# Causal attention with values and their remainders as one 128-column stationary operand, and the output stored tile by tile

## What is computed

```python
def nsa_attention(q_rope, q_plain, k_cmp, v_cmp, k_slc, v_slc, k_win, v_win, gates):
    ...
    def block(i):
        ...
        s_c = jnp.einsum('bghqd,bgcd->bghqc', qp, k_cmp)
        p_c = jax.nn.softmax(jnp.where(vis_c, s_c, -1e30), axis=-1) * vis_c.astype(f32)
        o_c = jnp.einsum('bghqc,bgcd->bghqd', p_c, v_cmp)
        ...
        s_s = jnp.einsum('bghqd,bgqkd->bghqk', qr, k_g)
        p_s = jax.nn.softmax(jnp.where(vis_s[:, :, None], s_s, -1e30), axis=-1)
        o_s = jnp.einsum('bghqk,bgqkd->bghqd', p_s, v_g)
        ...
        s_w = jnp.einsum('bghqd,bgkd->bghqk', qr, kw)
        p_w = jax.nn.softmax(jnp.where(vis_w, s_w, -1e30), axis=-1)
        o_w = jnp.einsum('bghqk,bgkd->bghqd', p_w, vw)
        return gt[..., 0:1] * o_c + gt[..., 1:2] * o_s + gt[..., 2:3] * o_w
...
def second_block(...):
    ...
        x_lat = x_lat + m_lat[:, 5] * rms_norm_2(sqrelu_mlp(h, mlp_w1[i], mlp_w2[i]), norm_g[i, 3])
    ...
    return x_lat
```

## Time and profile before

| | before |
|---|---|
| median of 3 runs | 3649.59 us (3646.3 to 3649.65) |
| the profiled execution | 3647.38 us, of which its span is 3645.6 us |
| TensorE matmuls | 3450.7 us busy, 95% of the span, 17972 instructions |
| TensorE weight loads | 2851.2 us, 78% |
| VectorE | 1940.6 us, 53% |
| ScalarE | 1360.0 us, 37% |
| GpSimd | 561.3 us, 15% |

### The profile page before, as it was taken

The page is one execution under the profiler, slowest core; times in us unless marked ns, Lnnn a source line. Parts: engine busy times, 40 slices in busy tenths (PEclk is TensorE's granted clock), DMA queues, the critical chain, the costliest instruction groups (busy, mean ns, idle before and its releaser), DMA issues. The chain is left out here.

```text
span 3645.6 us, 46669 instructions
## 1 busy us (share of the span) xinstructions
PE 3450.7 (95%) x17972; PEld 2851.2 (78%) x17972; DVE 1940.6 (53%) x2402; ACT 1360.0 (37%) x1991; POOL 561.3 (15%) x394
## 2 busy tenths in 40 slices
PE   6989999999998999999998999899999999999998
PEld 5766878888776687788876888788888788868886
DVE  4264348777526433877765652533333656654444
ACT  3266234444326623444433443312212344432222
POOL 0042004333104200333320110100000100000000
PEclk9999999999998999999998999999999999999999
DMA  3201234443220032344410001111111011112231
GB/s 127 84 1 58 93 105 145 157 158 115 88 84 1 35 105 93 131 158 160 150 52 18 18 12 70 47 58 65 62 59 68 24 68 52 55 35 93 92 102 60
DMA packets 59364, 287.77 MB, mean 79 GB/s; under 512 B 10704, under 2 KB 11984, under 8 KB 31952
## 3 DMA queue, kind: packets, MB, share of 16 engines
q1 hardware_dynamic: 59216, 285.77, 22.7%
HBM read 283.64 MB, written 2.10 MB: 78 GB/s over the span
## 5 line engine op out<-in xcount | busy, mean ns | idle before, releaser
L162 PE MATMUL ps<-h_hi,w_hi_rest 128*128 128x512 f32 (+1 forms) x1072 | 385.2, 359 | 4.6 <-DVE h_lo L386 4.6
L163 PE MATMUL ps<-h_lo,w_hi_rest 128*128 128x512 f32 (+1 forms) x1072 | 363.4, 354 | 0.0
L1343 POOL TENSOR_TENSOR ada_context<-ada_context,ada_scaled 128x768 f32<-128x768 f32 x112 | 287.5, 2567 | 455.2 <-ACT ada_scaled L1425 450.0
L165 PE MATMUL ps<-h_hi,w_lo_rest 128*128 128x512 f32 (+1 forms) x1072 | 322.0, 355 | 0.0
L151 DVE TENSOR_TENSOR w_lo_mix<-w_raw,w_hi_mix 128x2048 fp32r<-128x2048 f32 x94 | 217.1, 2309 | 185.4 <-ACT w_hi_mix L145 185.4
L425 POOL TENSOR_TENSOR x<-x,y 128x512 f32<-128x512 f32 (+1 forms) x32 | 64.5, 2016 | 1522.3 <-DVE y L431 1522.3
L162 PE MATMUL ps<-h_hi,w_hi_mix 128*128 128x512 f32 x736 | 287.0, 390 | 4.5 <-DVE w_lo_mix L151 2.3
L163 PE MATMUL ps<-h_lo,w_hi_mix 128*128 128x512 f32 x736 | 286.5, 389 | 0.0
L165 PE MATMUL ps<-h_hi,w_lo_mix 128*128 128x512 f32 x736 | 286.5, 389 | 0.0
L1507 DVE TENSOR_TENSOR y<-ps,y 128x512 f32<-128x512 f32 (+1 forms) x224 | 165.7, 751 | 216.1 <-PE ps L165 215.3
L145 ACT ACTIVATE w_hi_rest<-w_raw 128x2048 fp32r<-128x2048 f32 x81 | 154.5, 1908 | 326.7 <-PE ps L165 315.5
(11 more groups left out here) (397 smaller groups left out, 7739.6 us busy)
## 6 DMA issues: line engine op xcount, KB each, us to landing
w_raw<-in_stream SPq DMA_DIRECT2D x205, 1024.0 KB, 5.0
ada_raw<-in_ada_w SPq DMA_DIRECT2D x128, 384.0 KB, 5.1
cmp_w<-in_cmp_w SPq DMA_DIRECT2D x8, 1024.0 KB, 7.3
mla_raw<-in_stream SPq DMA_DIRECT2D x8, 512.0 KB, 3.7
x<-in_x SPq DMA_DIRECT2D x1, 2048.0 KB, 8.9
out<-x SPq DMA_DIRECT2D x1, 2048.0 KB, 7.3
x<-in_ctx SPq DMA_DIRECT2D x1, 1024.0 KB, 11.1
consts<-in_consts SPq DMA_DIRECT2D x1, 768.0 KB, 11.7
```

What stands on the lines that cost most here:

```text
L162: pe.matmul(out, whi, xhi, start=start, stop=False)
L163: pe.matmul(out, whi, xlo, start=False, stop=False)
L165: last = pe.matmul(out, wlo, xhi, start=False, stop=stop)
L1343: pool.tensor_tensor(ada.context, ada.context, ada.scaled[:, j % 2, :], ALU.add).then_inc(m["context"], 1)
```

## The change

Four edits. (1) The values and their remainders become one stationary operand `vp` of 128 columns, 64 of high part and 64 of remainder, and so `values` needs two matmuls a quarter instead of three; rows 0 to 63 of the bank gather what the high parts give, rows 64 to 127 what the remainders give. (2) The compressed branch alike: `pct` becomes F32R with 64 rows, the high part in rows 0 to 31 and the remainder in rows 32 to 63, and `vc_pack` is a stationary operand of the same 64 rows; VectorE makes the remainders in stage_cmp_attention. (3) Once a head the lower half of the bank is rounded into `low_half` by ScalarE (`round_low`) and added to the upper half by a matmul with the identity (`fold`); `head_high` moves two iterations back and `head_low` as well, from iteration 8k+6 to 8k+8. (4) Each of the 8 row tiles is stored by its own DMA as soon as it is added, inside the last residual stage. The diff, cut to its core:

```diff
--- before.py
+++ after.py
...
         k.sem(f"ca_{s}") for s in ("scored", "masked", "exp", "probs", "flipped", "chain"))
     q_hi, q_lo, k_hi, v_hi, v_lo = (k.sem(f"ca_{s}") for s in ("q_hi", "q_lo", "k_hi", "v_hi", "v_lo"))
+    copied, zeroed = k.sem("ca_copied"), k.sem("ca_zeroed")
+    low = slice(NCP, 2 * NCP)
+    def turned(t, g, rows):
+        a = t * 512 + 2048 * g
+        return (b.pct[rows, 4 * g:4 * g + 4, t * P:(t + 1) * P],
+                k.ps[0:NCP, a:a + 512].rearrange("p (h q) -> p h q", q=P))
...
+                pe.wait_ge(zeroed, 1)
                 pe.wait_ge(probs, t // 2 + 1)
                 for h in range(HEADS):
                     a = t * 512 + 2048 * (h // 4) + h % 4 * P
-                    last = pe.transpose(k.ps[0:NC, a:a + P], b.pc[:, t, h, 0:NC], k.c["ident"])
+                    last = pe.transpose(k.ps[0:NCP, a:a + P], b.pc[:, t, h, :], k.c["ident"])
                 last.then_inc(flipped, 1)
...
             normalise(1)
+            for t in range(QT):
+                for g in range(2):
+                    dve.wait_ge(copied, 2 * t + g + 1)
+                    dst, src = turned(t, g, low)
+                    hi, _ = turned(t, g, slice(0, NCP))
+                    dve.tensor_tensor(dst, src, hi.bitcast(F32), ALU.subtract)
...
             def copy(t):
                 act.wait_ge(flipped, t + 1)
                 for g in range(2):
-                    a = t * 512 + 2048 * g
-                    act.activation(b.pct[0:NC, 4 * g:4 * g + 4, t * P:(t + 1) * P],
-                                   k.ps[0:NC, a:a + 512].rearrange("p (h q) -> p h q", q=P), ACT.Copy)
+                    dst, src = turned(t, g, slice(0, NCP))
+                    act.activation(dst, src, ACT.Copy).then_inc(copied, 1)
...
-            act.activation(b.vhi, b.v, ACT.Copy).then_inc(v_hi, 1)
+            by_branch = b.v.rearrange("p t (r d) -> p t r d", d=64)
+            act.activation(b.vp[:, :, :, 0:64], by_branch, ACT.Copy).then_inc(v_hi, 1)
+            act.wait_ge(zeroed, 2)
+            act.activation(b.vcp[0:NC, 0:64], b.vc[0:NC, :], ACT.Copy).then_inc(v_hi, 1)
+            act.activation(b.vcp[NCP:NCP + NC, 0:64], b.vc[0:NC, :], ACT.Copy).then_inc(v_hi, 1)
...
         @block.gpsimd
         def _(pool):
+            pool.memset(b.pc[:, :, :, NC:NCP], 0.0).then_inc(zeroed, 1)
+            pool.wait_ge(zeroed, 1)
+            pool.memset(b.vcp.bitcast(F32), 0.0).then_inc(zeroed, 1)
+            pool.wait_ge(zeroed, 2)
             pool.wait_ge(v_hi, 1)
-            pool.tensor_tensor(b.vlo, b.v, b.vhi.bitcast(F32), ALU.subtract).then_inc(v_lo, 1)
-            pool.wait_ge(v_lo, 1)
+            pool.tensor_tensor(b.vp[:, :, :, 64:P], b.v.rearrange("p t (r d) -> p t r d", d=64),
+                               b.vp[:, :, :, 0:64].bitcast(F32), ALU.subtract).then_inc(v_lo, 1)
+            pool.wait_ge(v_hi, 3)
+            for n, rows in enumerate((slice(0, NC), slice(NCP, NCP + NC))):
+                pool.wait_ge(v_lo, n + 1)
+                pool.tensor_tensor(b.vcp[rows, 64:P], b.vc[0:NC, :], b.vcp[0:NC, 0:64].bitcast(F32),
+                                   ALU.subtract).then_inc(v_lo, 1)
+            pool.wait_ge(v_lo, 3)
             for h in range(HEADS):
                 own, other = head_rows(h)
                 pool.wait_ge(q_hi, h + 1)
...
@@ -866,18 +894,23 @@
                 if br == 0 and part == 0:
                     if h >= 2:
                         pe.wait_ge(s["lo_done"], h - 1)
-                    pe.matmul(k.ps[0:64, bank:bank + 512], b.vc[0:NC, :], b.pct[0:NC, h, :], start=True, stop=True)
+                    pe.matmul(k.ps[:, bank:bank + 512], b.vcp, b.pct[:, h, :], start=True, stop=True)
                 if part == 0:
                     pe.wait_ge(s["pt_lo"], QT * (u + 1))
-                out = k.ps[0:64, bank + j * P:bank + 512]
+                out = k.ps[:, bank + j * P:bank + 512]
                 hi, lo = b.pt[u % 2]
-                vhi, vlo = b.vhi[:, j, 64 * br:64 * br + 64], b.vlo[:, j, 64 * br:64 * br + 64]
-                pe.matmul(out, vhi, hi[:, j, j * P:SEQ], start=False, stop=True, skip_group_check=True)
-                pe.matmul(out, vlo, hi[:, j, j * P:SEQ], start=False, stop=True, skip_group_check=True)
-                last = pe.matmul(out, vhi, lo[:, j, j * P:SEQ], start=False, stop=True,
+                pe.matmul(out, b.vp[:, j, br, :], hi[:, j, j * P:SEQ], start=False, stop=True, skip_group_check=True)
+                last = pe.matmul(out, b.vp[:, j, br, :], lo[:, j, j * P:SEQ], start=False, stop=True,
                                  skip_group_check=True)
                 if j == 0:
                     last.then_inc(s["summed"], 1)
+            def fold(h):
+                bank = VALUES + (h % 2) * 512
+                pe.wait_ge(s["rounded"], h + 1)
+                pe.matmul(k.ps[0:64, bank:bank + 512], b.identr[64:P, 64:P], b.low_half[64:P, :], start=False, stop=True,
+                          skip_group_check=True).then_inc(s["folded"], 1)
...
             for i in range(AHEAD):
                 scores(i)
@@ -887,8 +920,11 @@
                 flips(i)
                 if i >= QT + 1:
                     values((i - QT - 1) // QT, (i - QT - 1) % QT)
+                if i % (2 * QT) == QT + 2 and i > 2 * QT:
+                    fold(i // (2 * QT) - 1)
...
                 values((i - QT - 1) // QT, (i - QT - 1) % QT)
+            fold(HEADS - 1)
...
                 if i + AHEAD < STEPS:
                     top(i + AHEAD)
                 low(i)
-                if i % (2 * QT) == QT + 2 and i > 2 * QT:
-                    head_low(i // (2 * QT) - 1)
+                if i % (2 * QT) == 0 and i > 2 * QT:
+                    head_low(i // (2 * QT) - 2)
+            head_low(HEADS - 2)
             head_low(HEADS - 1)
...
             def head_high(h):
                 bank, rows = VALUES + (h % 2) * 512, slice(64 * (h % 2), 64 * (h % 2) + 64)
+                act.wait_ge(s["folded"], h + 1)
+                act.activation(b.onhi[rows, h // 2, :], k.ps[0:64, bank:bank + 512], ACT.Copy).then_inc(s["hi_done"], 1)
...
+            def round_low(h):
+                bank = VALUES + (h % 2) * 512
                 act.wait_ge(s["summed"], 2 * h + 2)
-                act.activation(b.onhi[rows, h // 2, :], k.ps[0:64, bank:bank + 512], ACT.Copy).then_inc(s["hi_done"], 1)
+                act.activation(b.low_half[64:P, :], k.ps[64:P, bank:bank + 512], ACT.Copy).then_inc(s["rounded"], 1)
...
@@ -971,7 +1013,10 @@
                 if i + AHEAD < STEPS:
                     exps(i + AHEAD)
                 if i % (2 * QT) == QT + 1 and i > 2 * QT:
+                    round_low(i // (2 * QT) - 1)
+                if i % (2 * QT) == QT + 3 and i > 2 * QT:
                     head_high(i // (2 * QT) - 1)
+            round_low(HEADS - 1)
             head_high(HEADS - 1)
...
@@ -1529,6 +1574,16 @@
...
+        if store is not None:
+            stored = k.sem(f"{name}_stored")
+            @block.sync
+            def _(sp):
+                for t in range(KT):
+                    res.wait(sp, t)
+                    sp.dma_start(store[:, t, :], k.x[:, t, 0:SEQ]).then_inc(stored, 16)
+                sp.wait_ge(stored, 16 * KT)
...
-    stage_residual(nc, k, "mlp1r", c.y, SEQ, parts_of(b, 1, 3, SEQ), y_norm)
+    stage_residual(nc, k, "mlp1r", c.y, SEQ, parts_of(b, 1, 3, SEQ), y_norm, store=a["out"])
...
-    b.pct = at("pct", [NCP, HEADS, SEQ], F32, 157)
+    b.pct, b.vcp = at("pct", [2 * NCP, HEADS, SEQ], F32R, 157), at("vc_pack", [2 * NCP, P], F32R, 156)
...
-    b.vhi, b.vlo = at("v_hi", [P, QT, P], F32R, 137), at("v_lo", [P, QT, P], F32R, 139)
+    b.vp, b.low_half = at("v_pack", [P, QT, 2, P], F32R, 137), at("low_half", [P, SEQ], F32R, 149)
...
-        stored = sem("stored")
-        with nc.Block() as block:
-            @block.sync
-            def _(sp):
-                sp.dma_start(a["out"], k.x[:, :, 0:SEQ]).then_inc(stored, 16)
-                sp.wait_ge(stored, 16)
```

More of the change, by code:

```diff
@@ L1521, in stage_mlp, with stage_residual @@
     return last_u
-def stage_residual(nc, k, name, y, tok, post, norm, next_norm=None, next_unit=None, prefetch=None, reset=None, units=()):
+def stage_residual(nc, k, name, y, tok, post, norm, next_norm=None, next_unit=None, prefetch=None, reset=None, units=(), store=None):
     res = Residual(k, f"{name}_r", norm, k.x, post)
```

3 lines of the change are left out of this document (2 added, 1 removed).

## The result

| | before | after |
|---|---|---|
| median of 15 runs each, same comparison | 3646.24 us (3639.25 to 3650.1) | 3660.29 us (3653.54 to 3672.04) |
| profiled execution, its span | 3647.38, 3645.6 us | 3662.14, 3660.3 us |
| TensorE busy, its granted clock (1 is 2.4 GHz throughout) | 95%, 0.981 | 94%, 0.979 |

After over before is 1.0044, 95% interval 1.0035 to 1.0054: 14 to 16 us slower, where 1.3 us faster was reckoned for the same two executions. The new kernel also scatters more: its fastest run is 7 us above the median of before, its slowest 26.

A forecast was written before the change was run, and what follows sets the result against it. It took a serial ScalarE-VectorE chain, not TensorE, as the attention loop's bound. Store -4.9, compressed stage +2.4, loop +3.2, tail 0, half-clock stretch -2.0 summed to -1.3 us: median 3648.3 us, range 3636 to 3657.

The forecast's parts named there:

- The bound: Causal attention loop: a serial chain of ScalarE exponentials and VectorE reciprocals and maxima sets the pace; TensorE mostly waits.
- The plain unit: Causal loop, unit without head copies: 0.18 us shorter, to 5.17 us, 1.4 us gained a layer.
- The store: Span's end: storing each row tile once added gains 4.9 us, between 3.5 and 5.5.
- The compressed stage: stage_cmp_attention: added VectorE subtractions end behind ScalarE's copies, 2.4 us lost over both layers.
- The tail: End of the attention stage: added rounding copy and fold offset removed work; zero, at worst 0.6 us lost a layer.
- The half-clock stretch: Stretch at 1130 to 1140 us where TensorE is the bound: fewer matmuls gain 2.0 us once, between 0 and 4.
- The head's copies: Causal loop, units with copies: net 0.5 us lost, 6 times a layer; 1.6 us a layer after the plain-unit gain.
- Same size, same place: no change: ScalarE in the causal loop: round_low takes head_high's old place, so nothing is gained or lost there.
- The fold: TensorE, once a head: it waits for round_low with later scores queued behind, but their three-step lead makes it cost nothing.
- the leg of 3.56 us: Unit with copies, 256-wide to next 512-wide exponential: 0.82 us longer than 2.74; not near 3.56 would refute the prediction.
- without that slack: If scores did not run three steps ahead, the fold's wait on TensorE would cost some 0.3 us a head, 4 us.
- the clock falls: Rival: less-occupied TensorE drops to half clock for a quarter of both loops, costing 11 us: 3661; chance 0.10.

The follow-up runs named there:

- e_store_only: Kernel before with only the store by row tile added, attention unchanged: median 3642.3 us, ratio 0.9991.
- e_round_early: Changed kernel with the rounding copy put ahead of the 512-wide exponential of its step instead of behind it: median 3655.8 us, ratio 1.0028.
- e_no_fold: Changed kernel without the fold's matmul and its waits, output lacking the values' remainder half: median 3660.7 us, ratio 1.0035.
- e_filler: Changed kernel with a third matmul, against zeros, put back in each step of the values: median 3666.6 us, ratio 1.0055.
- look_filler: Second profile of e_filler, the changed kernel with the third matmul against zeros, unaltered: 3662.9 us.
- e_moved: Changed kernel with the rounding copy ahead of the 512-wide exponential and the head's two copies half a head later: median 3638.4 us, ratio 0.9976.
- e_head_moved: Changed kernel with only the head's two copies moved half a head later, rounding copy left behind its exponential: median 3647.3 us, ratio 1.0005.

## Why the prediction was wrong

*The bound* was read rightly. The loop is a chain through ScalarE and VectorE, and TensorE's share of 95% said little: all of line 876 taken out of the old kernel gave 0.33 us a head, where its duration is 1.16. "TensorE mostly waits" was too strong, since its matmuls are busy 56.9 of 60 us there.

*The plain unit*: 5.17 said, 5.16 measured; over a layer the units without copies gave 1.2 us where 1.4 was said. *The store*: 4.9 us said, 5.6 in the trace; the pieces kept up with the adds, and the last landed 2.4 us after the last add, under the 2.7 taken from the 256 KB load. The rule on batching DMAs ("DMA: Bandwidth & Descriptors", Bandwidth, in the Trainium skill) did not decide: pieces of 256 KB landed in 2.0 us each, beside work. *The compressed stage*: 2.4 said, 2.65 measured; the subtractions end at 204.89, 1.3 us behind the last copy. *The tail*: zero said; from the last unit's first exponential to the end of on_lo are 10.3 us before and 10.6 after, 0.3 us a layer. *The number of heads* was right: six units a layer carry copies between two exponentials, and the seventh lies in the tail.

*The half-clock stretch*: 2.0 said. Before loses 4.0 us to it in layer 2 (28.56 from the first score to the first on_lo, 24.59 in layer 1); after loses 0.3 there (28.16 against 27.86), since its stretch lay at the loop's very start (it begins at 1137.4, and 1137 to 1145 has a clock of 0.57). The gain of 3.7 in this pair is luck of where the stretch fell and not the working of the edit: e_store_only, with the old attention, loses nothing to it either (24.60).

*The head's copies* is the step that failed, and with it the sum: 1.6 us a layer was said and 5.5 measured without any fall of the clock, 7.8 us too little in two layers. A unit with copies grew by 1.07 us, from a mean of 5.86 to 6.93, where 0.50 was said, from 5.73 to 6.23. Three errors lie in it.

- The unit with copies was read in one place. Its leg after the 512-wide exponential was 1.46 us in that unit; the next one in the kernel before shows another kind, which its 283.38 start gives away (1.69 us behind 281.69, with 1.83 and 2.47 to follow):

```profile
283.38 0.57 ACT L950 ACTIVATE p<-ps,sst 128x384 f32<-128x384 f32 x1
285.21 0.47 ACT L950 ACTIVATE p<-ps,sst 128x256 f32<-128x256 f32 x1 [1.00 <-DVE sst L898]
287.68 0.69 ACT L950 ACTIVATE p<-ps,sst 128x512 f32<-128x512 f32 x1 [0.64 <-DVE sst L898]
```

 "Same size, same place: no change" for round_low thus kept a cost in every head that was there in every second one: its place between the 512 and the 384-wide exponential makes 1.70 of 1.46. e_round_early shows it: the leg went back to 1.46.
- The fold was put at nothing. In the first kind of unit ScalarE waits 0.21 us for line 903 behind it, pt_hi starts 1.26 us behind the 256-wide exponential and not 0.94, and the leg of 3.56 us measured 3.86. Without the fold it measured 3.53 (e_no_fold), so the steps of that leg were named and sized rightly and only this wait was missing: 0.33 us, the very 0.3 that the prediction gave as the price "without that slack".
- In the second kind the same leg is 4.11 with the fold and 4.06 without. There on_hi starts 0.59 and not 0.46 us behind the exponential, and the steps behind it take up to 0.1 us more each. Why is not shown; the kernel before has the two kinds too.

So the head went from 11.21 to 12.09, +0.88. Two of the prediction's own signs of being wrong were there: the leg of 3.56 us, and the clock in the loop.

*The clock* is the rest, and is the second thing missing. In the two profiled executions all terms are known: 5.6 gained at the store, 2.65 lost in the compressed stages, 2 x 5.5 in the loops, 5.4 by falls, 3.7 gained by the half-clock stretch, together +9.8 us, and +4.9 in code that the change doesn't touch make the 14.7. For the medians the account is looser. Without falls the change costs 2.65 + 11.0 - 5.6 = 8.0 us, or 3654.3 us, and the median is 6 us higher. Falls explain most of that: half-clock time in the loops took 1.9, 5.7 and 10.9 us in the three profiled executions, where of the two traces with the old attention before lost 4.0 and e_store_only nothing, and e_filler puts the falls at some 4 us. What remains, 2 us or so, is not shown. This was the rival "the clock falls", given 0.10 with 3661, on the evidence that 7.63 busy of 10 had kept a clock of 1.00. Ten microseconds at the end of a loop were no evidence on ninety. That the rival's 3661 is next to the measured 3660.3 is chance: it reckoned 11 us of falls, and more of the loss came from the copies.

Whether the missing work on TensorE is a condition of the falls is supported by e_filler and look_filler (no head hit in four loops, against hits in four of the changed kernel's six and a fall in the last head of a fifth), though the filler also moves when everything else runs. That it isn't enough is shown by e_moved, with the same work and no fall, and by e_head_moved, where TensorE is busy 52.3 of 60 us without a fall, against e_round_early, which has six falls and is busy 15.8 of 18.1 us (52.4 of 60) in a stretch at full clock. Which gap starts a fall stays open.

## What to carry to other kernels

Before work is moved within a loop, look for the engine's waits in it and put each copy into one of its own size: here ScalarE's two in waits of 0.65 us and VectorE's one in its waits of 0.4 cost 0.18 us a head together, and the same three in series with the chain, with the fold waiting for the first, cost 1.77. Read a periodic loop over two full periods of every kind before taking one as its base, by the start of one instruction that comes once a period. And when work is taken from an engine that isn't the bound, ask first what else its being busy was good for.

## What the runs showed of the hardware

The clock of TensorE can fall to half within a loop of steady work. It came back after 3.4 us in the steady heads of the changed kernel (0.87 and 0.79 in two windows of 5 us) and after 10 in e_round_early (0.60, 0.50 and 0.87 from 235 to 250). It fell in one execution and not in the next, with the same instructions: 1, 2 and 7 heads, all but one of them by 1.6 us. A median of such a kernel hides two effects, and the profile's heads at full clock separate them; one profile alone does not, since e_head_moved's slowest execution had no head hit and e_store_only's profile is its fastest execution, 9 us under its median. A fall is not tied to one wait: without the fold, and so without its wait of 0.93 us, it came in six heads.

The kernel before has heads of 11.46 and 10.95 us in turn, in every trace of it. The code of every head is the same but for the tiles' places, so a loop's period can be longer than its code suggests. What makes the two differ is not shown.
